# Hybrid decoder layer with a mixture of experts: the last three experts' outputs kept on chip, the other rows gathered in two groups

## What is computed

```python
hid = silu(einsum('nd,edf->nef', t, w_gate[gi])) * einsum('nd,edf->nef', t, w_up[gi])
y = y + einsum('nef,efd->nd', hid * combine[:, gi, :, None], w_down[gi])
...
x = x + g2 * hier_moe(h, ...)
return rms_norm(x, final_norm)
```

## Time and profile before

| what | us |
|---|---|
| median of 3 runs | 782.32 |
| lowest and highest | 781.32, 784.16 |
| the profiled execution | 781.9 |
| its span | 780.0 |
| mean granted TensorE clock | 0.946 |
| TensorE busy | 686.8 |
| VectorE busy | 318.2 |
| ScalarE busy | 180.0 |

### The profile page before, as it was taken

One profiled execution on the slowest core, in us unless ns is written; L12 is line 12 of the kernel. 1 busy time (PEld: TensorE's weight loads), 2 busy tenths in 40 slices (PEclk: granted clock), 3 DMA queues, 4 the chain that ended last, 5 costly groups with the idle time before them and its releaser, 6 DMA issues.

```text
span 780.0 us, 9903 instructions
## 1 busy us (share of the span) xinstructions
PE 686.8 (88%) x3851; PEld 401.5 (51%) x3851; DVE 318.2 (41%) x752; ACT 180.0 (23%) x434; POOL 116.7 (15%) x164
## 2 busy tenths in 40 slices
PE   1799899999999999879999985899999999999830
PEld 1674446667666697545654455444444544443210
DVE  3203657856466533786612228350211211202126
ACT  3204215122121121456711141020111211201103
POOL 8700122313032155000000000010000000000030
PEclk9989999999999999899999986999999999999975
DMA  9999003793330300750085047638999999999965
GB/s 332 375 264 364 3 1 108 245 294 109 108 108 1 52 5 7 266 216 2 1 324 108 28 179 280 195 110 349 375 423 413 405 413 409 390 404 410 421 208 201
DMA packets 75475, 173.62 MB, mean 223 GB/s; under 512 B 21954, under 2 KB 38940, under 8 KB 71836
## 3 DMA queue, kind: packets, MB, share of 16 engines
q1 hardware_dynamic: 69520, 157.59, 56.0%
q0 software_dynamic: 2672, 9.44, 3.5%
q10 hardware_dynamic: 3228, 5.84, 2.0%
HBM read 156.59 MB, written 16.26 MB: 222 GB/s over the span
## 4 chain that ended last, share of the span: by engine, by line
PE 76%; DVE 9%; POOL 4%; issue 4%; ACT 3%; DMA 3%; POOLq 0%; ACTq 0%; DVEq 0%
PE ps L1031 14%; PE ps L1153 7%; PE ps L1064 7%; PE ps L2300 7%; PE ps L2267 5%; PE ps L1025 4%; PE ps L1059 2%; PE ps L2378 2%; PE ps L2264 2%; PE ps L2384 2%; DMA expert_rows<-yo 2%; PE ps L2291 2%; POOL lev L1648 2%; PE ps L653 2%; PE ps L2388 2%
## 5 line engine op out<-in xcount | busy, mean ns | idle before, releaser
L1031 PE MATMUL ps<-gu,xgT 128*128 128x512 f32 x256 | 113.0, 600 | 3.6 <-DVE xgT L1110 2.5
L1031 PEld LDWEIGHTS ps<-gu,xgT 128*128 128x128 f32 x256 | 48.6, 192 | 63.2 <-issue 63.2
L2300 PE MATMUL ps<-hT,winr 128*128 128x512 f32 x144 | 72.6, 612 | 0.0
L1540 POOL DMA_INDIRECT xg<-xn_rows,list x15 | 13.9, 928 | 384.7 <-DVE list L1447 185.9
L1153 PE MATMUL ps<-wout,yT 128*128 128x512 f32 x128 | 57.6, 610 | 0.0
L1064 PE MATMUL ps<-dn,hidT 128*128 128x512 f32 x128 | 56.5, 594 | 0.0
L1753 POOL TENSOR_TENSOR cc<-low,lev 128x512 f32<-128x512 f32 x20 | 30.2, 1518 | 129.5 <-DVE low L2087 104.0
L1891 DVE SCALAR_TENSOR_TENSOR acc<-ada,st,acc 128x512 f32<-128x512 f32 x56 | 48.5, 866 | 1.3
L2267 PE MATMUL ps<-hT,wind 128*128 128x512 f32 x96 | 43.4, 605 | 0.0
L1025 PE MATMUL ps<-gu,xgT 128*32 128x256 f32 (+1 forms) x384 | 43.0, 452 | 0.0
L1153 PEld LDWEIGHTS ps<-wout,yT 128*128 128x128 f32 x128 | 24.6, 195 | 30.0 <-issue 30.0
(11 more groups left out here) (433 smaller groups left out, 1046.6 us busy)
## 6 DMA issues: line engine op xcount, KB each, us to landing
dn<-in_w_down SPq DMA_DIRECT2D x16, 2048.0 KB, 23.3
gu<-in_w_gate SPq DMA_DIRECT2D x15, 2048.0 KB, 21.5
gu<-in_w_up SPq DMA_DIRECT2D x15, 2048.0 KB, 26.0
ada<-in_w_ada SPq DMA_DIRECT2D x12, 2048.0 KB, 11.6
expert_rows<-zero SPq DMA_DIRECT2D x12, 512.0 KB, 6.7
expert_rows<-yo ACTq DMA_DIRECT2D x8, 512.0 KB
wout<-in_w_out SPq DMA_DIRECT2D x1, 3072.0 KB, 10.6
x<-in_x SPq DMA_DIRECT2D x2, 1024.0 KB, 6.2
```

The lines of the kernel that those rows point to most:

```text
L1031: ins = nc.tensor.matmul(PS[2 * b + w][:, :], T["xgT"][:, k, :], w_in[:, w, k, :], start=(k == 0), stop=(k == KT - 1))
L2300: ins = t.matmul(bank[:, :], w(k), T["hT"][:, k, :], start=(k == 0), stop=(k == KT - 1))
```

## The change

`ORDER` becomes 0, 1, 2, 12, 3, 11, 4, 10, 5, 9, 6, 8, 7, 13, 14, 15, in rows 128, 128, 128, 32, 128, 64, 128, 64, 128, 64, 128, 64, 128, 32, 32, 32. The last three positions (`on_chip`) store nothing: VectorE evicts each quarter of their `PS[4]` into 32 partitions of a new tile `yc`, whose first 32 partitions are cleared at the last position. Position 12 (`MID`) has a block of its own at the end of `expert_rows`; rows it doesn't use (`ZERO_ROW`) are filled with zeros by one more store early on.

A token's first row is now from positions 0 to 11, and is gathered when those are stored and gate and up of position 13 are done. Its second row may be from position 12 and is gathered when that is stored. Slots of on-chip experts point at the zero rows, with weight zero. VectorE adds `w1 y1` inside the loop, at position 14. At the end TensorE makes for each block of 128 tokens two products of a diagonal matrix of `w2` with `y2` and two of a one-hot matrix `back` (with the weights in it) with `yc`, in PSUM, and VectorE adds them to `x2`. `back` is made from `in_row` by four transposes and a copy at position 4. The conditions for extra tiles are put inside one outer condition.

```diff
-TILE_START = [sum(SIZES[:n]) for n in range(E - 1)]
-OTHER_ROWS = sum(SIZES[:E - 1]) + P * EXTRA
-TILE_START += [OTHER_ROWS] + [sum(SIZES[:E - 1]) + P * n for n in range(EXTRA)]
-ROWS = OTHER_ROWS + SIZES[E - 1]
 BIG = SIZES.count(P)
+CHIP = 3
+ORDER = list(range(NBUF))
+_big, _less = list(range(NBUF, BIG)), list(range(E - CHIP - 1, BIG - 1, -1))
+while _big:
+    ORDER += [_less.pop(0), _big.pop(0)]
+ORDER += _less + list(range(E - CHIP, E))
+MID = ORDER[E - CHIP - 1]
+EXTRA_ROW = sum(SIZES[:E - CHIP])
+MID_ROW = EXTRA_ROW + P * EXTRA
+CHIP_ROW = MID_ROW + SIZES[MID]
+ZERO_ROW = sum(SIZES[:MID])
+TILE_START = [MID_ROW if n == MID else sum(SIZES[:n]) for n in range(E - CHIP)]
+TILE_START += [CHIP_ROW + sum(SIZES[E - CHIP:n]) for n in range(E - CHIP, E)]
+TILE_START += [EXTRA_ROW + P * n for n in range(EXTRA)]
+ROWS = CHIP_ROW
+ONEHOT_AT = 3
...
+    at("yc", o + 4 * K, [P, D])
...
+    at("diag", o2 + 832, [P, ST, P])
...
+    at("back", o2 + 2 * K, [P, S])
...
-    ORDER = list(range(NBUF))
-    big, less = list(range(NBUF, BIG)), list(range(E - 2, BIG - 1, -1))
-    while big:
-        ORDER.append(less.pop(0))
-        ORDER.append(big.pop(0))
-    ORDER += less + [E - 1]
-    LAST = ORDER[-1]
...
+    def on_chip(n):
+        return E - CHIP <= n < E
+
     STORED = [1]
     for n in range(E + EXTRA):
-        STORED.append(STORED[-1] + P // rows_of(n))
+        STORED.append(STORED[-1] + (0 if on_chip(n) else P // rows_of(n)))
...
-        sp.wait_ge(sem("yo_zero"), 16 * EXTRA)
+        sp.wait_ge(sem("yo_zero"), 16 * (EXTRA + 1))
...
+    def pe_onehot(pe):
+
+        pe.wait_ge(sem("routing"), ROUTING["onehots"])
+        pe.wait_ge(sem("yo_d"), ONEHOT_AT + 1)
+        for i in range(ST):
+            ins = nc.tensor.transpose(PS[5][:, i * P:(i + 1) * P], T["in_row"][:, 0, i, :], idf[:])
+        ins.then_inc(sem("routing_pe"), 1)
+
+    def pe_back(pe):
+
+        pe.wait_ge(sem("routing"), ROUTING["route_i"])
+        pe.wait_ge(sem("exp_out"), 3)
+        for i in range(ST):
+            pe.wait_ge(sem(f"y_in{i}"), 16)
+            if i == 2:
+                pe.wait_ge(sem("yo_d"), E + 1)
+            for w in range(2):
+                nc.tensor.matmul(PS[2 * i + w][:, :], T["diag"][:, i, :], T["y2"][:, i, w * 512:(w + 1) * 512],
+                                 start=True, stop=False)
+            pe.wait_ge(sem("yo_d"), E + 1)
+            for w in range(2):
+                ins = nc.tensor.matmul(PS[2 * i + w][:, :], T["back"][:, i * P:(i + 1) * P],
+                                       T["yc"][:, w * 512:(w + 1) * 512], start=False, stop=True)
+            ins.then_inc(sem("oproj_mm"), 1)
...
+        if on_chip(n):
+
+            dve.wait_ge(sem("yo_d"), E - CHIP + 1)
+            dve.wait_ge(sem("xg_tr"), E)
+            if n == E - 1:
+                nc.vector.memset(T["yc"][0:32, :], 0.0)
+            to = slice(32 * (n - E + CHIP + 1), 32 * (n - E + CHIP + 2))
+            for w in range(4):
+                rows, c = slice(32 * w, 32 * w + 32), slice(256 * w, 256 * w + 256)
+                ins = nc.vector.tensor_tensor(T["yc"][to, c], PS[4][rows, 0:256], T["g2q"][rows, :], ALU.mult)
+            ins.then_inc(sem("yo_d"), 1)
+            return
...
-    def extras(eng, body):
+    def extra_count(eng):
 
         eng.wait_ge(sem("routing"), ROUTING["route_i"])
-        n_extra = eng.value_load(T["route_i"][0:1, 0:1], min_val=0, max_val=EXTRA)
-        for x in range(EXTRA):
-            with eng.If(n_extra > x):
-                body(x, E + x)
-        return n_extra
+        return eng.value_load(T["route_i"][0:1, 0:1], min_val=0, max_val=EXTRA)
+
+    def extras(eng, n_extra, body, last=None):
+
+        with eng.If(n_extra > 0):
+            for x in range(EXTRA):
+                with eng.If(n_extra > x):
+                    body(x, E + x)
+            if last:
+                last()
...
+            if n - 1 == ONEHOT_AT:
+                pe_onehot(pe)
+            if n - 2 == ONEHOT_AT:
+                pe.wait_ge(sem("exp_out"), 3)
             if n < E - 1:
                 pe_down(pe, n - 1)
         pe_hidden(pe, E - 1, 1)
         pe_down(pe, E - 1)
+        pe_back(pe)
+        n_extra = extra_count(pe)
...
+            if x == 0:
+                pe.wait_ge(sem("x3"), ST)
...
-            if n == E - 1:
-                act_output(act, n - 1)
             act_silu(act, n, b)
             if n + 1 < E:
                 act_rows(act, n + 1)
+            if n - 1 == ONEHOT_AT:
+                act.wait_ge(sem("routing_pe"), ROUTING_PE["list_mm"] + 1)
+                a.activation(T["back"][:], PS[5][:, :], ACT.Copy).then_inc(sem("exp_out"), 1)
+            if not on_chip(n - 1):
                 act_output(act, n - 1)
+            if n == 3:
+                n_extra = extra_count(act)
         act_hidden(act, E - 1, 1)
-        act_output(act, E - 1)
-
-        act.wait_ge(sem("yo_zero"), 16 * EXTRA)
 
         def extra(x, n):
             act_rows(act, n)
             act_silu(act, n, 0)
             act_hidden(act, n, 0)
+            if n == E:
+                act.wait_ge(sem("yo_zero"), 16 * (EXTRA + 1))
             act_output(act, n)
 
-        extras(act, extra)
+        extras(act, n_extra, extra, lambda: act.wait_ge(sem("x3"), 2 * ST))
+        a.activation(rden[:, 0:1], one, ACT.Sqrt)
...
-        link(v.tensor_scalar(t16, order, E - 1.5, float(OTHER_ROWS - sum(SIZES[:E - 1])), ALU.is_gt, ALU.mult))
+        link(v.tensor_scalar(t16, order, E - CHIP - 0.5, float(CHIP_ROW - EXTRA_ROW), ALU.is_gt, ALU.mult))
+        link(v.tensor_tensor(tile0, tile0, t16, ALU.add))
+        link(v.tensor_scalar(t16, order, float(MID), float(MID_ROW - ZERO_ROW), ALU.is_equal, ALU.mult))
         link(v.tensor_tensor(tile0, tile0, t16, ALU.add))
...
+        slotf, virtual, mine = T["slotf"][:], T["place"][:], T["first"][:]
+        link(v.tensor_scalar(virtual, slotf, 32.0 - CHIP_ROW, None, ALU.add))
+        for n, w in enumerate((w1, w2)):
+            for i in range(ST):
+                ins = v.tensor_scalar(T["in_row"][:, n, i, :], T["row_n"][:], virtual[:, n, i:i + 1], w[:, i:i + 1],
+                                      ALU.is_equal, ALU.mult)
+        link(ins)
+        v.tensor_tensor(T["in_row"][:, 0], T["in_row"][:, 0], T["in_row"][:, 1], ALU.add).then_inc(sem("routing"), 1)
+
+        link(v.tensor_scalar(mine, slotf, CHIP_ROW - 0.5, None, ALU.is_gt))
+        link(v.scalar_tensor_tensor(virtual, slotf, -float(ZERO_ROW), mine, ALU.add, ALU.mult))
+        link(v.tensor_tensor(slotf, slotf, virtual, ALU.subtract))
+        link(v.tensor_scalar(mine, mine, -1.0, 1.0, ALU.mult, ALU.add))
+        link(v.tensor_tensor(w1, w1, mine[:, 0], ALU.mult))
+        link(v.tensor_tensor(w2, w2, mine[:, 1], ALU.mult))
...
-        link(v.tensor_scalar(t16, order, float(LAST), None, ALU.is_equal))
-        link(v.tensor_tensor(T["s16"][:], T["M1"][:], t16.unsqueeze(1).broadcast_to([P, ST, E]), ALU.mult))
-        link(v.tensor_reduce(swap, T["s16"][:], AX.X, ALU.add))
+        link(v.tensor_scalar(swap, T["slotf"][:, 0, :], MID_ROW - 0.5, None, ALU.is_gt))
...
+        link(v.tensor_copy(T["route_i"][:, 0:1 + EXTRA], T["rf"][:, 0:1 + EXTRA]))
+        for i in range(ST):
+            ins = v.tensor_scalar(T["diag"][:, i, :], idf[:], w2[:, i:i + 1], None, ALU.mult)
+        ins.then_inc(sem("routing"), 1)
+        n_extra = extra_count(dve)
...
+            if n == E - 2:
+
+                dve.wait_ge(sem("y1_in"), 16 * ST)
+                for i in range(ST):
+                    x = T["x2"][:, i, :]
+                    ins = v.scalar_tensor_tensor(x, T["y1"][:, i, :], w1[:, i:i + 1], x, ALU.mult, ALU.add)
+                link(ins)
         dve_output(dve, E - 1)
+        for i in range(ST):
+            dve.wait_ge(sem("oproj_mm"), ST + i + 1)
+            for w in range(2):
+                x = T["x2"][:, i, w * 512:(w + 1) * 512]
+                ins = v.tensor_tensor(x, PS[2 * i + w][:, :], x, ALU.add)
+            ins.then_inc(sem("x3"), 1)
...
-        n_extra = extras(dve, extra)
-
-        dve.wait_ge(sem("y1_in"), 16 * ST)
-        with dve.If(n_extra > 0):
+        def extra_rows_back():
...
             dve.wait_ge(sem("y1_in"), 2 * 16 * ST)
-        for i in range(ST):
-            x = T["x2"][:, i, :]
-            ins = v.scalar_tensor_tensor(x, T["y1"][:, i, :], w1[:, i:i + 1], x, ALU.mult, ALU.add)
-        link(ins)
...
+        extras(dve, n_extra, extra, extra_rows_back)
         dve.wait_ge(sem("fn_in"), 16)
-        for i in range(ST):
-            x = T["x2"][:, i, :]
-            dve.wait_ge(sem(f"y_in{i}"), 16)
-            v.scalar_tensor_tensor(x, T["y2"][:, i, :], w2[:, i:i + 1], x, ALU.mult, ALU.add).then_inc(sem("x3"), 1)
...
-            g.indirect_dma_start(T[f"y{n + 1}"][:, i, :], None, yo_d if n else yo_d[0:OTHER_ROWS, :],
+            g.indirect_dma_start(T[f"y{n + 1}"][:, i, :], None, yo_d if n else yo_d[0:MID_ROW, :],
...
```

(29 more changed lines are left out.)

23 lines of the change are left out of this document (22 added, 1 removed).

## The result

The changed kernel takes **786.69 us** (median of 17 runs, 782.57 to 791.12). The kernel before, run beside it, takes 778.07 us (17 runs, 773.32 to 784.16). The ratio is **1.0107, interval 1.0084 to 1.0130**: slower by 1.1%. The range 773.5 to 787.3 holds the measured value, the case that was called likeliest does not.

The account below looks back on a forecast made before the run. TensorE and the weight stream are full together until about 730 us, then a chain of waits bounds. Start 9.1 us later, 23.9 instead of 34.0 behind it: 1.0 us shorter, 780.9, median 781.3 us; range 773.5 to 787.3.

Parts of the forecast that it names:

- the case that was called likeliest: Whole kernel: within 0.5%, as the shorter tail is paid back by late rows on VectorE and late weights; chance 0.50.
- 14 follow at 7.03 / 16 = 0.43: 6.0 at the full clock: Tail, after the evictions: 14 of 16 TensorE products behind the first two, 0.43 us each, 6.0 us together.
- the four transposes of the one-hot rows: TensorE: four products a quarter as wide as the 16 taking 7.03 us, 0.11 each, adding 0.5 us.
- the faster case: Weights set the last down product's start, which runs at full clock: 776.5 us, or 773.5; chance 0.33.
- store of position 11: Ahead of the first gather: issued at 717.1, lands in 7 us, between 3.77 and 11.01 seen; gather at 724.1.
- first rows at VectorE: Inside the loop: first gathered rows, sharing queues with the weights, land at 747.3 us while VectorE waits from about 736.
- last weights landed: Weight stream: the remaining 0.96 MB share with the second gather and land at 752.0 us, 7.9 later than before.
- last down product starts: TensorE: starts at 755.1 instead of 746.0, after first rows, additions 4.9, evictions 1.7, product and handing over 1.2.
- branch of VectorE on the path: Tail: one branch over all twelve extra experts, hidden behind the last additions; 0 us, bounds 0 and 3.7.
- The reorder: New expert order: TensorE 10.3 us late from position 7, regained at the end; later buffers hidden by the load backlog.
- The slower clock: Tail: TensorE stays at the lower clock for the 14 products, 12.0 instead of 6.0 us: 787.3 us; chance 0.13.
- The long turns between the queues: DMA queues: rows wait for nine weight packets once more, landing 5.2 us later: 786.5 us; chance 0.04.

Follow-up runs that it names:

- the late additions: Changed kernel with the four additions of the first rows moved behind the product of the last position: 781.26 us, 1.0046 to the kernel before.
- held-back gathers: The best division tried, with the first gather waiting for gate and up of the last position: 781.49 us, 1.0025 to the kernel before.
- The profile with the four products: The best division tried, plus four unread products ahead of the last down product: 774.65 us, 0.9945 to the kernel before.
- the best division tried: Changed kernel with late additions, earlier clearing, VectorE adding second rows of blocks 0, 2, 3; TensorE keeps block 1's diagonal pair: 776.05 us, 0.9983 to the kernel before.

## Why the prediction was wrong

**The step that failed** is the last one of the sum, "14 follow at 7.03 / 16 = 0.43: 6.0 at the full clock". The row counts instructions in the profile, the 14 were counted in the code. The row of 7.03 us belongs to the down product of a 128-row expert, whose code is four hidden blocks by two halves: 8 products, `x16` in the profile. A product costs 0.86 us; 14 of them 12.0 us; measured from 761.14 to 773.46: 12.3. Of the 6.7 us that the tail came out longer than predicted, 6.3 are this term. With 12.0 in place of 6.0 the same sum gives 785.0 us of span, which is what the profile has, and 787.3 us, where 786.69 was measured. The row by itself didn't show the error; the row beside the loop of the kernel before did: the 32-row form has 16 products in the code and `x32` in the earlier trace rows as well.

The same row priced the four transposes of the one-hot rows at 0.5 us, and there it did no harm: a transpose is recorded as one instruction (`x4` for four at line 1083), and they hold TensorE for 0.59 us. So a count of two can't be carried over to every operation of TensorE either.

One small sum is off as well: in the faster case 0.96 MB at 0.41 MB/us behind 747.3 land at 749.6 and not at 749.2. It moves the lower end of the range by 0.4 us and nothing else.

Point by point, predicted and measured:

| step | predicted | measured |
|---|---|---|
| store of position 11 | 7 us, first gather at 724.1 | 8.9 us from 716.50, gather at 725.38 |
| first rows at VectorE | 747.3 | 746.59 |
| last weights landed | 752.0 | 749.2 (issued 727.56, 21.6 us) |
| last down product starts | 755.1 | 754.43 |
| its duration and clock | 3.9, half | 3.64, 0.50 |
| clearing of `yc` | 0.5 | 0.91 |
| four evictions | 1.7 | 1.73 |
| first of the 14 products, behind the down product's end | 2.3 | 3.1 |
| 14 products | 6.0 | 12.3 |
| from the last additions to the end | 10.3 | 10.3 (774.75 to 785.0) |
| branch of VectorE on the path | 0 | 0.02 |

**The start** was right in its size and its cause. VectorE's additions ahead of its work for TensorE decided: 5.5 of 9.3 us, shown by the late additions. That the weights reckoned for 752.0 would be in time was right too; they came 2.8 us earlier. How the queues shared between 729 and 745 us:

```profile
q1 hardware_dynamic: 566, 3.95, 59.4%
...
q0 software_dynamic: 560, 2.08, 32.3%
q10 hardware_dynamic: 144, 0.52, 8.1%
```

These are packets, MB and share of the engines of the changed kernel. The two queues passed equal numbers of packets (566 and 560), as assumed. From 724 to 749.2 the queue of the gathers moved 2.95 MB, close to what the sum has it move by the landing of the weights (2.10 + 0.96). What the sum had wrong is how far the weights were: it left 4.19 MB of gate and up of position 15 to be moved from 728.2 on, and q1 moved only 3.05 MB from there to 739.1, when TensorE could start on them (741.7 in the sum). So the weight stream was about 1.1 MB ahead of the reckoning.

**The reorder** taken as hidden: in the changed kernel nothing speaks against it, and held-back gathers give the start of before to 0.1 us with the new order in place. In the kernel before it isn't hidden (5 to 7 us), by a mechanism that the prediction named for another row, the single `yo` and its stores.

**The rivals.** The slower clock gave 787.3 us by 12.0 instead of 6.0 us for the 14 products. The number is met, the mechanism is not: the granted clock was 1.00 in that stretch, with the diagonal products of the first block filling the wait for the evictions. Where they are taken away, the mechanism does appear, for 1.8 us. The long turns between the queues would have brought the first rows 5.2 us later than reckoned; they came 0.7 earlier. (Equal numbers of packets alone don't tell how long a turn is.) The faster case is excluded by the first rows at 746.59, which set the start and not the weights. So the 0.50 for no change was a wrong price and not a wrong chain; with the right price the same chain forecasts slower.

The base moved as well: against the median of 782.32 the measured time is 0.6% more, against the 17 runs beside it 1.1%.

**What stays open.** That the missing 3.7 us at the start are bytes and not turns between queues was not tried by itself. The profile with the four products has its last down product 262.3 us behind the first expert, later than the 259.4 of the kernel it comes from. 1.7 us of it are the four products, as told above; the weights themselves landed 1.3 us later by the same mark, and whether that is more than scatter is open. Every split of a few us rests on one profile for each kernel. And the cause of the scatter ahead of the experts wasn't looked into. It goes with the clock only in part: before 520 us the lower level holds for 51.2 us in the first profile of the kernel before and for 61.4 us in the second, whose first expert starts 2.4 us later; but the first profile of the changed kernel and the one with late additions both have 47.8 us of it, and their first experts start 2.9 us apart.

## What to carry to other kernels

Price an operation by the same unit on both sides: set the count of a profile row beside the loop that issued it before dividing its time. Here one float32 product of the code was two instructions of the profile, and the error was the whole miss. Work brought forward into a queue stands ahead of all that is behind it: the same four additions cost 5.5 us ahead of the last product's operand and nothing behind it. When work is moved between a busy engine and a waiting one, check both: the best division tried left TensorE the pair of products that keeps it running through its wait, and gave VectorE the rest in its gaps. And work put into a wait only to fill it must end before the wait does.

## What the runs showed of the chip that was not expected

- A float32 product of 128x512 is recorded as two instructions and takes 0.86 us at the full clock: 7.03 us for 8 products, 12.3 for 14, 3.60 for 4, and 1.72 for each pair. A 128x128 transpose is recorded as one.
- Four products that nobody reads, 3.60 us, ahead of a product that waits for its weights, brought that product from 3.64 to 1.93 us. In the profile taken they ended 1.7 us after the weights had landed, so that the start lost what the duration gained.
- An idle stretch of 3.31 us of TensorE was followed by 3.8 us at a granted clock of 0.55; the changed kernel, with products in that stretch, had 1.00.
- Clearing 32 x 1024 elements on VectorE takes 0.91 us, twice one eviction of 256 columns.
- The start of the first expert scatters by 6.5 us between profiles of one and the same code ahead of it (485.7 to 492.2 us), so differences of a few us are to be read from a mark inside the profile, or from ten runs and more.
